# A two-layer block with product-key experts: gathered groups of rows shared out anew over the steps of the expert stage

## The chip, the cores and the metric

One core of a Trainium2 chip. Times are device microseconds of one execution. Where a profiled execution is used, its span (first to last instruction) and its own time are given. The engines are TensorE (PE in the profile, its weight loads PEld), VectorE (DVE), ScalarE (ACT), GpSimd (POOL) and SyncE (SP), each with its own instruction stream, run in order; they meet at semaphores.

## The reference

Two blocks follow each other on x [512 tokens, 1024]. Each has a mixer (gated linear attention in the first; retention and stick-breaking attention in the second) and then an expert layer (PEER). The change touches only how the expert layers are ordered in time:

```
q      = (h @ w_q)  per head and half                 # 8 heads, 2 halves of 128
top 16 of each half's scores against 128 sub-keys     # -> 256 candidates, best 16
expert = first_key * 128 + second_key                 # 16384 experts, 128 choices a token
act    = gelu(x . u[expert]) * softmax(best)
y      = sum over the 128 choices of act * v[expert]
```

u and v are float32 tables of 16384 x 1024 (64 MB each), one pair a layer.

## The kernel before

The four tiles of 128 tokens are treated in two ways. **Dense tiles** (2 and 3, 256 tokens): all of u and v is streamed once, as 128 blocks e of 128 experts (512 KB of u and 512 KB of v each, by SP). `first_product` (L747, matmuls at L753) multiplies block e of u with the tokens into one of two PSUM banks; ScalarE's `block_gelu` (L1206, L1211) takes it out; VectorE's `weigh_pair` (L1796, L1804) multiplies it with the tokens' gates for these experts, two blocks at a time; `second_product` (L757, L763) adds it to y in PSUM. The gates come from matmuls over one-hot rows: `gates_of_batch` (L773, L789) makes those of four tokens for a quarter of the blocks (64 batches a quarter). For each batch ScalarE's `hit_batch` (L1213, L1221 and L1224) spreads the second key, in quarter 0 every other batch is spread by VectorE's `second_keys` (L1786, L1792); for each four batches VectorE's `first_keys` (L1772, L1780 and L1782) spreads the first key, and ScalarE's `copy_gates` (L1226, L1231) copies four batches' result to SBUF.

**Gathered tiles** (0 and 1): each of a token's 128 choices is fetched by an indirect DMA from GpSimd (L2046, 128 rows of 4 KB), four choices a group. A u group (`score_rows`, L1851) takes four dot products on VectorE; `group_gelu` on ScalarE (L1234, L1237) follows; a v group (`add_rows`, L1862 and L1871) adds four weighted rows. There are 64 of each, 128 units in all a layer, u and v in turn; each kind has a ring of 6 rows, a slot of which is fetched again once VectorE has read it.

**The order** is written out by step tables. Before step 0 quarter 0's 64 batches run, with 24 first products (`EARLY`) and the first `FIRST_UNITS` units (one behind every fifth batch, `first_units`). Then 128 steps: at step e TensorE does first product e + 16 (`AHEAD`; from e = 8 until e = 111), second product e, and the batches up to `batches_due(e)` (192 are left). VectorE at step e does `weigh_pair(e + 4)` on even e, the first keys up to `spreads_due(e)`, one piece of the choice of tile 1's experts (steps 8 to 48), and the units up to `units_due(e)`. ScalarE at step e does the group gelus of VectorE's step e - 1, block gelu e + 15, the hits up to `batches_due(e + 1)` and the copies up to `copies_due(e)`. Hits have a ring of 4, the first keys' spreads a ring of 2, both freed by TensorE's batches. `first_product(e)` waits for block gelu e - 2.

`unit_table` (L135) gives `units_due`: from step 8 on, units in proportion to a share of TensorE's time in the step less VectorE's other work in it.

Of the kernel before, what the change touches and what calls it, by code (L numbers as in the profile page):

```python
# [23 lines left out]
NH, TOPK, NKEY = 8, 16, 128  # L24
# [8 lines left out]
BATCHES = ND // BATCH  # L33
WIDE = 16
WIDES = ND // WIDE
AHEAD = 16
EARLY = 24
# [6 lines left out]
GROUPS = SLOTS // RING  # L44
# [36 lines left out]
def by_scalar(q, n):  # L81

    return q > 0 or n % 2 == 0
# [13 lines left out]
PAIR_PIECES = 8  # L97
PIECES = 5 * PAIR_PIECES + 1
EXP_PIECE = PIECES - 5
FIRST_UNITS = 11  # L100
SHORT_UNITS = 5
LATER = (QUARTERS - 1) * BATCHES


def batches_due(e):

    return 0 if e < 0 else min(LATER, 2 * e + 4 + min(8, e // 2))


def spreads_due(e):  # L110

    return 0 if e < 0 else -(-batches_due(e + 1) // 4)


def copies_due(e):

    return 0 if e < 0 else min(LATER // 4, e // 2 + 3, batches_due(e + 1) // 4)
# [7 lines left out]
def pieces_due(e):  # L125

    return max(0, min(PIECES, e + 1 - (EARLY - AHEAD)))


def first_units(n):  # L130

    return max(0, min(FIRST_UNITS, n // 5))


def unit_table():  # L135

    room = []
    for e in range(NKEY - 2):
        pe = 3.45 * (1 + (EARLY <= e + AHEAD < NKEY)) + 0.37 * (batches_due(e) - batches_due(e - 1))
        other = 0.45 + 1.69 * (spreads_due(e) - spreads_due(e - 1)) + 1.25 * (pieces_due(e) - pieces_due(e - 1))  # L140
        room.append((pe, other))
    share = ((4 * GROUPS - FIRST_UNITS) * 5.15 + sum(v[1] for v in room)) / sum(v[0] for v in room)
    done, table = 0.0, []
    for pe, other in room[EARLY - AHEAD:]:
        done += max(0.0, share * pe - other)
        table.append(done)
    short = [FIRST_UNITS + (e + 1) * SHORT_UNITS // (EARLY - AHEAD) for e in range(EARLY - AHEAD)]
    return short + [short[-1] + round((4 * GROUPS - short[-1]) * v / done) for v in table]


UNITS = unit_table()


def units_due(e):

    return FIRST_UNITS if e < 0 else UNITS[min(e, len(UNITS) - 1)]


def unit(n):

    if n in (0, 4 * GROUPS - 1):
        return ("u", 0) if n == 0 else ("v", 2 * GROUPS - 1)
    return ("u", (n + 1) // 2) if n % 2 else ("v", n // 2 - 1)
# [49 lines left out]
def build(nc, a, out, mod_dram, x_dram, two_pi):  # L213
    with ExitStack() as ctx:
# [782 lines left out]
        def _(act):  # L997
# [208 lines left out]
            def block_gelu(layer, e):  # L1206
                at = layer * NKEY + e
                if e >= len(zg_first) + ZG:
                    act.wait_ge(blk_summed, at - ZG + 1)
                act.wait_ge(blk_done, at + 1)  # L1210
                nc.scalar.activation(zg(e), ps[4 + e % 2][:, 0:ND], ACT.Gelu).then_inc(blk_gelu, 1)  # L1211
# [41 lines left out]
            def unit_gelu(layer, u):  # L1253
                kind, g = unit(u)
                if kind == "u":
                    group_gelu(layer, g)

            def dense_acts(layer):
# [12 lines left out]
                for e in range(blocks_before(BATCHES - 5), EARLY):  # L1271
                    block_gelu(layer, e)
                for u in range(first_units(BATCHES - 6), FIRST_UNITS):
                    unit_gelu(layer, u)
# [92 lines left out]
        def _(dve):  # L1367
# [367 lines left out]
            def peer(layer):  # L1735
# [36 lines left out]
                def first_keys(q, m):  # L1772

                    at = (layer * QUARTERS + q) * WIDES + m
                    c = slice(m * WIDE, (m + 1) * WIDE)
                    if at >= 2:
                        dve.wait_ge(ga_used, 4 * (at - 1))
                    shape = [P, WIDE // BATCH, QA, BATCH]
                    of_keys = lambda v: v.rearrange("p (g t) -> p g t", t=BATCH).unsqueeze(2).to_broadcast(shape)
                    spreads(tt(hot_one, key_rows, of_keys(first_no[q][:, c]), ALU.is_equal))  # L1780
                    for r in range(3):
                        last = tt(hot[m % 2][:, r], hot_one, of_keys(g_part[:, r, c]), ALU.mult)  # L1782
                    last.then_inc(ga_ready, 1)
                    dve.wait_ge(ga_ready, at + 1)

                def second_keys(n):  # L1786

                    at = layer * QUARTERS * BATCHES + n
                    if at >= HITS:
                        dve.wait_ge(ga_used, at - HITS + 1)  # L1790
                    shape = [P, BATCH, P]
                    tt(hits[n % HITS].rearrange("p (j k) -> p j k", j=BATCH), keyno16.unsqueeze(1).to_broadcast(shape),  # L1792
                       second_no[:, n * BATCH:(n + 1) * BATCH].unsqueeze(2).to_broadcast(shape), ALU.is_equal)\
                        .then_inc(hit_by_vector, 1)

                def weigh_pair(e):  # L1796

                    at = layer * NKEY + e
                    q, j = divmod(e, QA)
                    if j == 0:  # L1800
                        dve.wait_ge(ga_copied, (layer * QUARTERS + q + 1) * WIDES)
                    dve.wait_ge(blk_gelu, at + 2)
                    z = zg_pair(e)
                    tt(z, z, gates[q % 2][:, j:j + 2, :, :], ALU.mult).then_inc(blk_ready, 2)  # L1804

                chooser = tile_experts(1)
                for n in range(BATCHES):
                    if n % 4 == 0:
                        first_keys(0, n // 4)
                    if not by_scalar(0, n):  # L1810
                        second_keys(n)
                    for u in range(first_units(n - 1), first_units(n)):
                        run_unit(layer, u)
                for e in range(0, WEIGHED, 2):
                    weigh_pair(e)
                for e in range(NKEY):
# [18 lines left out]
            def run_unit(layer, n):  # L1835
                kind, g = unit(n)
                if kind == "u":
                    score_rows(layer, g)
                else:
                    add_rows(layer, g)  # L1840
                    if g % GROUPS == GROUPS - 1:
                        finish_tile(layer, g // GROUPS, y)

            def score_rows(layer, g):

                at = layer * 2 * GROUPS + g
                for b in range(RING):
                    n = RING * at + b
                    row = ur[n % ROWS]
                    dve.wait_ge(u_in[n % ROWS], 16 * (n // ROWS + 1))  # L1850
                    nc.vector.tensor_tensor_reduce(out=row, in0=row, in1=hn[:, g // GROUPS, :], scale=1.0, scalar=0.0,  # L1851
                                                   op0=ALU.mult, op1=ALU.add, accum_out=a8[g % 2][:, b:b + 1])\
                        .then_inc(u_free, 1)

            def add_rows(layer, g):

                at = layer * 2 * GROUPS + g
                if layer == 0 and g == 0:
                    dve.wait_ge(ada_stored, 16 * 12)
                c = g // GROUPS * SLOTS + g % GROUPS * RING  # L1860
                dve.wait_ge(act_out, at + 1)
                tt(c8[g % 2], g8[g % 2], gate[:, c:c + RING], ALU.mult).then_inc(c8_ready, 1)  # L1862
                dve.wait_ge(c8_ready, at + 1)
                for b in range(RING):
                    n = RING * at + b
                    row = vr[n % ROWS]
                    dve.wait_ge(v_in[n % ROWS], 16 * (n // ROWS + 1))
                    if g % GROUPS == 0 and b == 0:
                        last = ts(y, row, c8[g % 2][:, b:b + 1], None, ALU.mult)
                    else:  # L1870
                        last = stt(y, row, c8[g % 2][:, b:b + 1], y, ALU.mult, ALU.add)  # L1871
                    last.then_inc(v_free, 1)
                    dve.wait_ge(v_free, n + 1)

            def finish_tile(layer, t, y):

                if t in GATHERED:
                    dve.wait_ge(gathered_x_back, 32 * (layer + 1))
                if layer == 0:
                    tt(x[:, t, :], x[:, t, :], y, ALU.add).then_inc(x_ready, 1)  # L1880
                    dve.wait_ge(x_ready, t + 1)
                else:
                    dve.wait_ge(gate_in, 16)
                    step(tt(ysum, y, rows[:, 2, :], ALU.mult))
                    tt(x[:, t, :], x[:, t, :], ysum, ALU.add).then_inc(out_ready, 1)
                    dve.wait_ge(out_ready, t + 1)

            peer(0)
            dve.sem_inc(dve_to_act, 1)

# [129 lines left out]
            for t in range(NT):  # L2020
# [7 lines left out]
                rstd(1, D, t)  # L2028
                normed_tile(t, rows[:, 1, :], mod[:, 3, :])
            peer(1)  # L2030


# [59 lines left out]
```

## Time and profile before

| | us |
|---|---|
| median of 3 runs | 3321.93 (3318.65 to 3331.39) |
| the profiled execution's own time | 3318.72 |
| its span | 3316.9 |
| busy: PE, DVE, ACT, POOL | 3078.7, 2420.3, 1340.9, 1326.1 |
| HBM read | 921.87 MB, 280 GB/s over the span |

The span has two expert stages: layer 0's steps from 691.4 to 1628.8 us and layer 1's from 2367.5 to 3306.3 us, each behind about 110 us in which quarter 0's gates are made. PE's busy time counts matmuls from start to end, and they overlap, so 100% is a queue without gaps and not the peak rate. PEclk is the granted clock as a share of full speed. A row such as `[1.07 <-ACT big L1211]` says that the engine sat idle for 1.07 us before and what ended it.

### The profile page before, as it was taken

What the parts mean: (1) busy time and instruction counts of PE and PEld (TensorE: products, weight loads), DVE (VectorE), ACT (ScalarE), POOL (GpSimd) and SP (SyncE); (2) the same over time, 40 slices, a digit from 0 to 9 for tenths busy, and PEclk for the clock granted to TensorE, in tenths of its full rate; (3) what the DMA queues carried; (4) which work ended last, traced back from release to release, by engine and by line L of the source; (5) the groups of instructions that cost most, each with busy time, mean ns of one, the idle gap of its engine ahead of it and who ended that gap; (6) DMA issues with size and microseconds to landing.
All of it is one profiled execution on the core that took longest, in us unless ns stands there. A gap on an engine that the chain in (4) does not pass through costs nothing. (4 is left out here: it accounts for less than half of the span.)

```text
span 3316.9 us, 45880 instructions
## 1 busy us (share of the span) xinstructions
PE 3078.7 (93%) x16440; PEld 2049.9 (62%) x16440; DVE 2420.3 (73%) x5311; ACT 1340.9 (40%) x3417; POOL 1326.1 (40%) x1040
## 2 busy tenths in 40 slices
PE   7999899889999999988699999998899999999887
PEld 2466488656666666655344565787666666666553
DVE  5874459988889878777721253499888888878777
ACT  3232122786555555400111153226866565555000
POOL 0000000655556767766300000005456656767664
PEclk9999999999999999999899989999999999999999
DMA  8510261989999999999812101518799999999998
GB/s 302 181 51 26 95 228 65 347 291 364 374 371 376 409 409 409 409 408 409 332 57 82 49 22 38 195 67 310 276 359 376 384 353 409 409 409 409 409 409 351
DMA packets 282682, 931.22 MB, mean 281 GB/s; under 512 B 31804, under 2 KB 32460, under 8 KB 281944
## 3 DMA queue, kind: packets, MB, share of 16 engines
q0 software_dynamic: 147840, 536.96, 41.6%
q1 hardware_dynamic: 134616, 391.34, 31.3%
q8 instruction: 131, 2.15, 0.3%
q14 instruction: 95, 0.78, 0.1%
HBM read 921.87 MB, written 6.32 MB: 280 GB/s over the span
## 5 line engine op out<-in xcount | busy, mean ns | idle before, releaser
L753 PE MATMUL psum<-hT,mod 128*128 128x256 f32 x4096 | 969.8, 392 | 64.0 <-ACT big L1211 38.6
L753 PEld LDWEIGHTS psum<-hT,mod 128*128 128x128 f32 x4096 | 782.2, 195 | 189.7 <-issue 86.7
L1221 ACT ACTIVATE levels<-key_numbers,hT 128x128 bf16<-128x128 f32 x1792 | 566.7, 389 | 138.0 <-PE psum L789 137.5
L1871 DVE SCALAR_TENSOR_TENSOR tmp<-w,small,tmp 128x1024 f32<-128x1024 f32 x339 | 435.7, 1285 | 82.3 <-DMA w<-in_peer_v,tmp 37.8
L2046 POOL DMA_INDIRECT w<-in_peer_u,tmp x172 | 236.4, 1374 | 584.2 <-DVEq L1702 447.3
L1851 DVE CUSTOM_DVE_ANT_0 w<-w,hn 128x1024 f32<-128x1024 f32 x342 | 408.7, 1224 | 73.5 <-DMA w<-in_peer_down,tmp 36.2
L2046 POOL DMA_INDIRECT big<-in_peer_down,tmp x86 | 117.5, 1366 | 720.0 <-DVEq L1702 633.7
L763 PE MATMUL psum<-rows,big 128*128 128x512 f32 x768 | 344.2, 592 | 3.3 <-DVE big L1804 3.3
L789 PEld LDWEIGHTS psum<-x,levels 128*128 128x128 bf16 x6144 | 225.7, 101 | 164.8 <-issue 100.9
L1224 ACT ACTIVATE levels<-levels 128x512 bf16<-128x512 bf16 x448 | 282.2, 630 | 14.2
L789 PE MATMUL psum<-x,levels 128*128 128x32 bf16 x6144 | 236.9, 196 | 50.5 <-DVE levels L1792 25.7
L1231 ACT ACTIVATE big<-psum 128x512 f32<-128x512 f32 x128 | 137.3, 1072 | 343.3 <-PE psum L789 323.1
L2046 POOL DMA_INDIRECT w<-in_peer_down,tmp x170 | 224.5, 1321 | 117.0 <-DVE small L1851 73.7
L2046 POOL DMA_INDIRECT w<-in_peer_v,tmp x172 | 215.5, 1253 | 130.0 <-DVE tmp L1871 88.0
L2046 POOL DMA_INDIRECT w<-in_peer_up,tmp x170 | 214.0, 1259 | 119.6 <-DVE tmp L1871 78.5
L1871 DVE SCALAR_TENSOR_TENSOR tmp<-big,small,tmp 128x1024 f32<-128x1024 f32 x169 | 217.1, 1285 | 40.4 <-DMA big<-in_peer_up,tmp 18.1
L1237 ACT ACTIVATE small<-small 128x4 f32<-128x4 f32 x128 | 26.0, 203 | 537.1 <-DVE small L1851 537.0
L763 PEld LDWEIGHTS psum<-rows,big 128*128 128x128 f32 x768 | 145.6, 190 | 154.1 <-issue 150.0
L1851 DVE CUSTOM_DVE_ANT_0 big<-big,hn 128x1024 f32<-128x1024 f32 x170 | 203.9, 1223 | 30.9 <-DMA big<-in_peer_u,tmp 15.3
L763 PE MATMUL psum<-srow,big 128*128 128x512 f32 x384 | 173.0, 593 | 2.3 <-DVE big L1804 2.3
L763 PE MATMUL psum<-tmp,big 128*128 128x512 f32 x384 | 172.6, 592 | 0.0
L740 PE MATMUL psum<-hT,w 128*128 128x256 f32 x640 | 144.8, 379 | 0.0
(328 smaller groups left out, 4179.7 us busy)
## 6 DMA issues: line engine op xcount, KB each, us to landing
mod<-in_uT SPq DMA_DIRECT2D x256, 512.0 KB, 6.8
rows<-in_peer_v SPq DMA_DIRECT2D x64, 512.0 KB, 6.8
rows<-in_peer_up SPq DMA_DIRECT2D x64, 512.0 KB, 6.8
w<-in_w_in SPq DMA_DIRECT2D x14, 2048.0 KB, 8.5
srow<-in_peer_v SPq DMA_DIRECT2D x32, 512.0 KB, 6.9
tmp<-in_peer_v SPq DMA_DIRECT2D x32, 512.0 KB, 6.8
srow<-in_peer_up SPq DMA_DIRECT2D x32, 512.0 KB, 6.8
tmp<-in_peer_up SPq DMA_DIRECT2D x32, 512.0 KB, 6.8
```

Of the source, the lines that this page charges most:

```text
L740: last = nc.tensor.matmul(bank[:, 0:2 * P], w[:, k, c * P:(c + 1) * P], hT[:, k, tokens], start=k == 0, stop=k == KC - 1)
L753: last = nc.tensor.matmul(ps[4 + e % 2][:, 0:ND], ub[e % UV][:, k, :], hT[:, k, ND:SEQ], start=k == 0, stop=k == KC - 1)
L763: last = nc.tensor.matmul(y_dense[n][:, c * 512:(c + 1) * 512], zg(e)[:, n * P:(n + 1) * P], vb[e % UV][:, c * 512:(c + 1) * 512], start=e ...
L789: last = nc.tensor.matmul(ps[6 + n // 4 % 2][:, t * QA:(t + 1) * QA], hits[n % HITS][:, j * P:(j + 1) * P], hot[n // 4 % 2][:, r, n % 4, : ...
L1221: last = nc.scalar.activation(hits[n % HITS][:, j * P:(j + 1) * P], keyno, ACT.Abs, bias=nibT[:, n * BATCH + j:n * BATCH + j + 1])
L1224: nc.scalar.activation(hits[n % HITS], hits[n % HITS], ACT.Relu, scale=-1.0, bias=1.0).then_inc(hit_ready, 1)
L1231: nc.scalar.activation(gates[q % 2][:, :, 2 * m:2 * m + 2, :], ps[6 + m % 2].rearrange("p (j i a) -> p a j i", a=QA, i=8), ACT.Copy).then_ ...
L1237: nc.scalar.activation(g8[g % 2], a8[g % 2], ACT.Gelu).then_inc(act_out, 1)
L1851: nc.vector.tensor_tensor_reduce(out=row, in0=row, in1=hn[:, g // GROUPS, :], scale=1.0, scalar=0.0, op0=ALU.mult, op1=ALU.add, accum_out= ...
L1871: last = stt(y, row, c8[g % 2][:, b:b + 1], y, ALU.mult, ALU.add)
L2046: nc.gpsimd.indirect_dma_start(ring[n % ROWS], None, table, bass.IndirectOffsetOnAxis(idx[:, c:c + 1], 0))\
```

## The change

Three edits. The lead of the batches over two a step grows by one each four steps and not each two, so it reaches 8 at step 32 and not 16. One more unit is placed ahead of step 0; a loop is added for those that the batches' loop leaves over. And the units from step 8 on are shared out by a new measure: the smaller of TensorE's time in the step less VectorE's other work (with 0.53 us for weighing, not 0.45), and TensorE's time less 1.28 us for each dense block that is transferred.

```diff
-FIRST_UNITS = 11
+FIRST_UNITS = 12
...
-    return 0 if e < 0 else min(LATER, 2 * e + 4 + min(8, e // 2))
+    return 0 if e < 0 else min(LATER, 2 * e + 4 + min(8, e // 4))
...
 def unit_table():
-    room = []
-    for e in range(NKEY - 2):
-        pe = 3.45 * (1 + (EARLY <= e + AHEAD < NKEY)) + 0.37 * (batches_due(e) - batches_due(e - 1))
-        other = 0.45 + 1.69 * (spreads_due(e) - spreads_due(e - 1)) + 1.25 * (pieces_due(e) - pieces_due(e - 1))
-        room.append((pe, other))
-    share = ((4 * GROUPS - FIRST_UNITS) * 5.15 + sum(v[1] for v in room)) / sum(v[0] for v in room)
+    short = [FIRST_UNITS + (e + 1) * SHORT_UNITS // (EARLY - AHEAD) for e in range(EARLY - AHEAD)]
     done, table = 0.0, []
-    for pe, other in room[EARLY - AHEAD:]:
-        done += max(0.0, share * pe - other)
+    for e in range(EARLY - AHEAD, NKEY - 2):
+        blocks = 1 + (e + AHEAD < NKEY)
+        pe = 3.45 * blocks + 0.37 * (batches_due(e) - batches_due(e - 1))
+        other = 0.53 + 1.69 * (spreads_due(e) - spreads_due(e - 1)) + 1.25 * (pieces_due(e) - pieces_due(e - 1))
+        done += max(0.0, min(pe - other, pe - 1.28 * blocks))
         table.append(done)
-    short = [FIRST_UNITS + (e + 1) * SHORT_UNITS // (EARLY - AHEAD) for e in range(EARLY - AHEAD)]
     return short + [short[-1] + round((4 * GROUPS - short[-1]) * v / done) for v in table]
...
                     for u in range(first_units(n - 1), first_units(n)):
                         run_unit(layer, u)
+                for u in range(first_units(BATCHES - 1), FIRST_UNITS):
+                    run_unit(layer, u)
                 for e in range(0, WEIGHED, 2):
                     weigh_pair(e)
```

What the tables give, worked out from the code:

| after step | units before | after | batches before | after |
|---|---|---|---|---|
| ahead of 0 | 11 | 12 | 0 | 0 |
| 8 | 17 | 18 | 24 | 22 |
| 16 | 24 | 26 | 44 | 40 |
| 24 | 30 | 34 | 60 | 58 |
| 32 | 37 | 42 | 76 | 76 |
| 48 | 51 | 57 | 108 | 108 |
| 90 | 97 | 102 | 192 | 192 |
| 111 | 121 | 122 | 192 | 192 |
| 125 | 128 | 128 | 192 | 192 |

## Rows read from the trace of the kernel before

**Rows 1.** The page's 40 slices of the span: GB/s moved in each.

```profile
GB/s 302 181 51 26 95 228 65 347 291 364 374 371 376 409 409 409 409 408 409 332 57 82 49 22 38 195 67 310 276 359 376 384 353 409 409 409 409 409 409 351
```

**Rows 2.** Stretches of layer 0's stage: busy us of engines, clock, DMA share, GB/s.

```profile
580.00:691.40 111.40, 92.21 (x1038) 80.02 (x1037) 104.50 (x191) 78.41 (x198) 68.96 (x54) 0.94 0.91 336
691.40:740.40 49.00, 42.73 (x334) 24.17 (x334) 40.38 (x71) 45.63 (x122) 26.27 (x19) 0.97 0.75 270
740.40:1056.60 316.20, 311.86 (x1982) 214.74 (x1981) 271.39 (x596) 195.20 (x519) 182.91 (x141) 1.00 0.97 370
...
808.70:871.00 62.30, 62.30 (x398) 42.93 (x397) 57.14 (x131) 41.33 (x112) 41.14 (x32) 1.00 1.00 391
...
1056.60:1391.40 334.80, 328.52 (x2018) 225.70 (x2017) 274.83 (x396) 185.05 (x498) 236.18 (x179) 0.99 1.03 408
1391.40:1565.70 174.30, 154.25 (x537) 100.84 (x536) 128.35 (x162) 9.39 (x34) 113.14 (x96) 0.94 1.03 409
```

**Rows 3.** Waits, total us, times, longest; first 1056.6 to 1391.4, then to 1628.8.

```profile
PE psum L753 <- ACT big L1211: 6.3, 2, 3.2
...
PE psum L753 <- ACT big L1211: 10.4, 2, 8.7
PE psum L753 <- ACT hT L1211: 9.7, 2, 8.7
PE psum L763 <- DVE big L1804: 3.3, 4, 2.0
...
ACT small L1237 <- DVE small L1851: 212.6, 16, 16.3
```

**Rows 4.** Waits of VectorE from 740.4 to 1056.6 us.

```profile
DVE x L1780 <- PE psum L789: 34.0, 12, 6.9
```

**Rows 5.** Timeline of TensorE: start, us, line, operation, count; regular steps and the last product.

```profile
921.57 3.70 PE L753 MATMUL psum<-hT,mod 128*128 128x256 f32 x16
925.10 3.60 PE L763 MATMUL psum<-tmp,hT 128*128 128x512 f32 x8
928.53 0.93 PE L789 MATMUL psum<-x,levels 128*128 128x32 bf16 x24
929.30 3.70 PE L753 MATMUL psum<-hT,mod 128*128 128x256 f32 x16
...
1405.95 3.60 PE L763 MATMUL psum<-rows,big 128*128 128x512 f32 x8
...
1412.84 3.60 PE L763 MATMUL psum<-rows,big 128*128 128x512 f32 x8
...
1621.59 3.60 PE L763 MATMUL psum<-tmp,big 128*128 128x512 f32 x8
```

**Rows 6.** Waits of TensorE, 740.4 to 1056.6, and timelines around one of them.

```profile
PE psum L753 <- ACT hT L1211: 2.6, 2, 1.5
PE psum L753 <- ACT big L1211: 1.8, 2, 1.1
...
762.01 3.69 PE L753 MATMUL psum<-hT,mod 128*128 128x256 f32 x16 [1.07 <-ACT big L1211]
...
760.60 1.06 ACT L1231 ACTIVATE big<-psum 128x512 f32<-128x512 f32 x1 [5.00 <-PE psum L789]
```

**Rows 7.** Timeline of TensorE: a late stall.

```profile
1303.70 5.38 PE L753 MATMUL psum<-hT,mod 128*128 128x256 f32 x16 [3.04 <-ACT big L1211]
```

**Rows 8.** Timeline of VectorE: start of a u group, end of the v group behind it.

```profile
788.65 1.20 DVE L1851 CUSTOM_DVE_ANT_0 w<-w,hn 128x1024 f32<-128x1024 f32 x1
...
796.51 2.60 DVE L1871 SCALAR_TENSOR_TENSOR tmp<-w,small,tmp 128x1024 f32<-128x1024 f32 x2
```

**Rows 9.** Timeline of TensorE in step 0: one of seven batches that wait.

```profile
699.40 0.55 PE L789 MATMUL psum<-x,levels 128*128 128x32 bf16 x12 [1.28 <-ACT levels L1224]
```

**Rows 10.** Timeline of VectorE: the last spreads of quarter 0 and the first weighing.

```profile
683.74 1.29 DVE L1792 TENSOR_TENSOR levels<-key_numbers,hT 128x512 bf16<-128x512 bf16 x2
689.26 3.00 DVE L1804 TENSOR_TENSOR x<-x,big 128x512 f32<-128x512 f32 x3 [4.22 <-issue]
```

## The prediction

> **What bounds the kernel now.** I read the slices first [rows 1]: from slice 8 and again from slice 29 GB/s climbs from about 350 to 409 and stays there. These are the two expert stages, one per layer, some 1,050 us each of the 3317. The table by stage [rows 2] splits layer 0's stage at its steps: start of step 0 (691.4), 8 (740.4), 48 (1056.6), just before step 91 (1391.4), step 112 (1565.7) and the end (1628.8). In steps 8 to 47 TensorE is busy throughout and DMA moves 370 GB/s; from step 48 on DMA moves 408 to 409, two thirds of a layer's stage, and TensorE falls to 154 of 174 us. So the first third is paced by TensorE with transfers to spare, and the rest by transfers. The waits say the same [rows 3]: after step 91 ScalarE waits 212.6 of 237 us for VectorE's last scored row (it runs the group's gelu in order, ahead of the block gelu that frees TensorE's bank), and TensorE then waits for ScalarE's block gelu. VectorE itself waits for rows to land. From step 8 to 47 there are no such waits; there VectorE waits 34.0 us for TensorE's gate batches [rows 4].
>
> **TensorE's chain, to price things.** A step with two products and two batches is 7.73 us (921.57 to 929.30), one without batches 6.89 (1405.95 to 1412.84), a second product alone 3.43 (925.10 to 928.53), a batch 0.385 (half of what stands between 928.53 and 929.30) [rows 5]. From step 8: 83 x 7.73 + 21 x 6.89 + 16 x 3.43 + 2 odd batches x 0.385 = 842 us, so it could end at 740.4 + 842 = 1582.4. Its last second product begins at 1621.59 [rows 5] and ends at 1625.1. Of the 42.7 us lost, 4.4 are four short stalls before step 17 (2.6 and 1.8 in all, the longest 1.5 [rows 6]); 38.3 come late: 29.7 us of waits [rows 3], the rest slow matmuls after them: 16 take 5.38 us after a wait of 3.04, against 3.69 after 1.07 [rows 6, 7].
>
> **The share of groups.** A group of four gathered rows is 4 x 128 x 4 KB = 2.097 MB, 5.13 us at 409 GB/s; a dense block is 0.524 MB. The code's tables give, after step 48, 77 groups before and 71 after the change. Needed at 409 GB/s, against TensorE's time:
> - steps 49 to 90: before 46 groups, 140.5 MB, 343.6 us against 324.7: 18.9 over; after 45: 13.8 over.
> - steps 91 to 111: before 24 groups, 72.4 MB, 176.9 against 144.7: 32.2 over; after 20: 11.7 over.
> - steps 112 on: before 7, 1.4 over; after 6, 3.7 under.
>
> Before 52.5 over, of which 38.3 were lost: 14.2 is swallowed by the lead that the engines have over each other. After 21.8 over; less 14.2 leaves 7.6. That is -30.7 us, six groups times 5.13. Bounds: nothing gained (if the six can't be moved earlier) and -38.3 (if no late stall is left).
>
> Can steps 8 to 47 take five groups more (34 become 39; the sixth runs before step 0)? DMA: 370 GB/s x 316.2 us is 117.0 MB, plus 10.5 is 127.5 MB in about 326 us (TensorE's longer chain, below): 391 GB/s, under the 408 to 409 that it holds for 509 us [rows 2]. VectorE: a pair of groups takes from 788.65 to 796.51 + 2.60, so 5.2 us each, a little of it other work between them [rows 8]; 271.4 busy us plus 5 x 5.2 are 297 of 326, and the extra comes out of the 34.0 us for which it waits for TensorE anyway [rows 4]. It fits, with 9% to spare, tightest around step 16 (57.1 of 62.3 us now in steps 16 to 23 [rows 2]; one to two groups more fill it).
>
> At this place the Trainium skill speaks against the change: DMA: Bandwidth & Descriptors, section "Where 436 GB/s comes from", says that for transfers between HBM and SBUF the memory side binds at about 358 GB/s per core. By that the middle (370) would be full already, and the groups moved would only move the queue. The trace disagrees with 409 held for 509 us [rows 2], so the sum doesn't use it; a softer ceiling of that kind is rival 3.
>
> **The gates' lead.** Half of the extra batches now comes later: two fewer up to step 7 (19, not 21) and at step 8 (22, not 24). Before step 8 TensorE's batches wait for ScalarE, which spreads one each 1.83 us (a batch of 0.55 behind a wait of 1.28) and is busy 45.6 of 49 us [rows 2, 9]. Two fewer: -3.7 us; between that and 0, if something else paces; I take -3.7.
> The price: a gate copy on ScalarE waits for the fourth batch of its set. Where that batch falls in TensorE's next step, the copy (1.06 us) and the gelu behind it end after TensorE wants the bank: at 760.60 the copy runs after 5.00 us of waiting, and TensorE's next product starts 1.07 us late [rows 6]. The code's tables give this for 4 copies from step 8 on before (the products that follow, in steps 11, 13, 14 and 16, are the four stalls of 4.4 us in all), and for 13 after, up to step 32. At 1.1 each: +9.9 us. Bounds: the least and the most of the four, 0.7 (1.8 less the 1.1 beside it) and 1.5 [rows 6], give +4.7 to +15.1. Batches only deferred cost nothing more: 0.385 us each wherever they stand. VectorE's spreads follow the batches and are as many.
>
> **The twelfth group.** It is a scored one (u), at batch 60; the added loop behind the batches is then empty, so it does nothing. Its four rows (4.6 us) stand ahead of VectorE's spreads for batches 61 and 63, which end at 685.0 now [rows 10], and TensorE wants them from 686.4. After: 61 at about 689.1, 63 at 689.7, the batches end 2.2 us later than now, and with them the copy and the first weighing (689.26), before which VectorE idles 4.22 us [rows 10]. +2.2 us; bounds 0 (cover of 4.22) and 4.6. Queued behind it: ScalarE's group gelu and the first hits. Its gather of 2.1 MB lies where DMA moves 336 GB/s [rows 2].
>
> **Sum.** Per layer -30.7 - 3.7 + 9.9 + 2.2 = -22.3 us. From the bytes: unused now 316.2 x (409 - 370)/409 = 30 us in steps 8 to 47, after 326 x (409 - 391)/409 = 14; that is -16, with -5.1 for the group ahead and -1.5 for step 8 coming earlier: -22.6. I take -20 (VectorE at 91% will not fit without friction). Layer 1's slices, from 29 on, are those of layer 0 [rows 1], so the same again: -40 us. The profiled execution took 3318.72 (span 3316.9, 1.8 around it): 3279; the median of the runs is 3.2 above it: 3282.
>
> **Rivals.**
> 1. No late stall is left: singles instead of the double-group steps (steps 77, 87, 94 and 102 take two; the long stalls come one to three steps later, as at 1303.70 before step 80 [rows 7]) end them altogether, and with them the slow matmuls. -38.3 + 8.4 = -30 a layer: 3262. For it: the new table has no double after step 79. Against: 21.8 us of transfers are still over.
> 2. VectorE becomes the bound in steps 8 to 47: its waits for TensorE [rows 4] are ordering and don't shrink. 297 + 37 = 334 against 326: 8 us a layer go, and 2 more for the late product: -10 a layer: 3302. For it: steps 16 to 23 at 92% [rows 2].
> 3. Transfers top out near what steps 8 to 47 show (370 to 391 GB/s [rows 2]) while TensorE is fed too; no byte moves early. Then 9.9 + 2.2 - 3.7 = +8 a layer: 3338. Against: 409 stands beside a TensorE busy 328 of 335 us.
> 4. The other side: the 13 copy stalls grow with VectorE's fuller queue. One mechanism: ScalarE's copy waits a step, VectorE's late group behind it makes the stall 3 us, and matmuls go slow as at 1303.70 [rows 7]: 3.04 + 1.69 = 4.7 each, 13 x 4.7 - 4.4 = +57, less 30.7 and 1.5: +25 a layer: 3372. It decides from 13 c - 4.4 = 32.2, that is c = 2.8 us a stall; the four seen are 0.7 to 1.5.
>
> **How the numbers follow.** Forecast 0.50, rival 1 0.17, rival 2 0.18, rival 3 0.05, rival 4 0.06, and 0.04 that all cancel near no change. Under 0.5% (16.6 us) from 3322 a measurement can't tell from no change: faster is below 3305, slower above 3339. Faster: forecast, rival 1, most of rival 2: 0.82. Same: 0.11. Slower: 0.07. The range takes rival 1 and rival 2 in: 3256 to 3308.
>
> **What would show it.** Right: GB/s about 390 in steps 8 to 47 and TensorE's late waits under 15 us a layer; step 8's second product within 3 us of 740.4; some 13 waits of TensorE for ScalarE of about 1.1 us up to step 32; ScalarE's 212.6 us wait for VectorE far smaller; first weighing 2 us later. Wrong: VectorE waiting for landings before step 48, 5.38 us products before step 32, or DMA under 380 in the middle with the late stalls unchanged.

## The result and the profile after

Median of five runs 3300.36 us (3296.57 to 3302.62) against 3321.93 before (3318.65 to 3331.39, five runs): ratio 0.9928, 95% interval 0.9915 to 0.9941. The forecast was 3282 us and a gain of 40 us. The gain is 21.6 us between the medians, and 24 us by the ratio: as forecast in direction and inside the range, but little more than half in size. The profiled executions have spans of 3300.2 and 3316.9 us (before).

First GB/s in the page's 40 slices after the change, to lay beside [rows 1]:

```profile
GB/s 293 193 42 36 96 209 79 339 291 395 379 380 395 403 409 409 409 409 409 314 56 83 36 35 39 179 77 296 283 391 375 370 398 400 409 408 409 409 409 336
```

Then layer 0's stage after, cut at the same steps as in [rows 2] (starts of step 0, 8, 48, just before 91, 112, and TensorE's end); the columns are busy us of the engines with counts, granted clock, DMA share, GB/s:

```profile
697.30:743.90 46.60, 41.59 (x309) 23.30 (x308) 36.93 (x57) 42.15 (x114) 23.60 (x19) 0.96 0.76 269
743.90:1074.00 330.10, 314.12 (x2006) 216.13 (x2006) 296.40 (x636) 197.84 (x530) 203.08 (x159) 1.00 1.00 387
1074.00:1407.20 333.20, 327.31 (x2018) 224.75 (x2017) 274.87 (x392) 184.31 (x498) 230.39 (x180) 0.99 1.02 408
1407.20:1566.40 159.20, 152.91 (x537) 100.08 (x536) 112.43 (x144) 9.25 (x32) 100.72 (x83) 0.98 1.03 409
1566.40:1621.50 55.10, 55.10 (x129) 24.13 (x127) 38.89 (x45) 2.04 (x6) 19.11 (x16) 1.00 0.82 324
```

Steps 8 to 47 now move 387 GB/s (370 before) and VectorE is busy 296.4 us in them (271.4): the five groups went in, at almost exactly the 127.5 MB and 297 us of the forecast (387 x 330.1 = 127.8 MB). But the stretch takes 330.1 us, not the 326 forecast and the 316.2 before. The last stretch, 55.1 us at 324 GB/s, is new too: TensorE doesn't wait there any more, and the transfers idle for (409 - 324)/409 x 55.1 = 11 us.

TensorE's waits after: first in 743.9 to 1074.0, then in 1074.0 to 1407.2, then from 1407.2 on, there with ScalarE's wait for VectorE (total us, times, longest). They answer to [rows 6] and [rows 3]:

```profile
PE psum L750 <- ACT big L1208: 12.3, 10, 1.5
PE psum L750 <- ACT hT L1208: 3.6, 3, 1.5
...
PE psum L750 <- ACT big L1208: 4.6, 1, 4.6
...
PE psum L750 <- ACT big L1208: 6.3, 3, 3.1
ACT small L1234 <- DVE small L1850: 166.4, 12, 18.1
```

There are 13 short waits, 15.9 us, where 4 took 4.4; each layer has them. The late waits fell from 29.7 us to 12.2 in layer 0 (4.6 and 6.3 as shown, and 1.3 once before batches at 1334, for which the profile names no releaser) and from 30.3 to 13.7 in layer 1, and ScalarE's wait for VectorE's last row from 212.6 to 166.4 us.

What each layer's stage took, stretch by stretch, read off the timelines of TensorE and VectorE (first row of u scored, starts of second products 0, 8, 48, 91 and 112, end of the last; last column: the last group's end against TensorE's):

| us | first u row to step 0 | steps 0-7 | 8-47 | 48-90 | 91-111 | 112-127 | last group |
|---|---|---|---|---|---|---|---|
| before, layer 0 | 100.7 | 48.9 | 316.2 | 342.5 | 166.7 | 59.4 | +3.6 |
| before, layer 1 | 100.7 | 48.9 | 317.9 | 340.2 | 169.3 | 58.3 | +4.1 |
| changed, layer 0 | 104.7 | 46.7 | 330.0 | 340.9 | 151.5 | 55.1 | -7.4 |
| changed, layer 1 | 104.7 | 46.7 | 331.7 | 339.7 | 152.9 | 55.1 | -7.1 |

Before, the last group ended a stage, now TensorE does, so a layer's stage is 9 us shorter, not 5: to TensorE's end 1034.4 became 1028.9 us and 1035.3 became 1030.7, and 3.6 to 4.1 us of a group behind it are gone. Both stages together give 17.7 us, and the end of layer 1 another 2.5 (tile 1 is finished ahead, not behind). Of that 3.5 us are lost again in work that the change does not touch, 1.7 ahead of layer 0's first u row and 1.8 between the stages; so the two spans differ by 16.7.

### The profile page after: what moved, and what is told of

Read it like the earlier page. It is cut to its first block and busy times, and to the rows that moved or that the text cites. A ratio compares the mean times of both kernels' runs of the same rounds, so it can differ in the third digit from the quotient of the medians.

```text
span 3300.2 us, 45872 instructions
## 1 busy us (share of the span) xinstructions
PE 3081.3 (93%) x16440; PEld 2052.6 (62%) x16440; DVE 2418.4 (73%) x5311; ACT 1338.2 (41%) x3417; POOL 1304.0 (40%) x1040
## 3 DMA queue, kind: packets, MB, share of 16 engines
q8 instruction: 131, 2.15, 0.3%
## 5 line engine op out<-in xcount | busy, mean ns | idle before, releaser
L1221 ACT ACTIVATE levels<-levels 128x512 bf16<-128x512 bf16 x448 | 282.2, 630 | 14.2
L1870 DVE SCALAR_TENSOR_TENSOR tmp<-big,small,tmp 128x1024 f32<-128x1024 f32 x169 | 217.2, 1285 | 43.8 <-DMA big<-in_peer_up,tmp 22.3
L2045 POOL DMA_INDIRECT w<-in_peer_up,tmp x170 | 203.1, 1195 | 115.0 <-DVE tmp L1870 76.0
```

What stands on the lines that cost most here:

```text
L1221: nc.scalar.activation(hits[n % HITS], hits[n % HITS], ACT.Relu, scale=-1.0, bias=1.0).then_inc(hit_ready, 1)
L2045: nc.gpsimd.indirect_dma_start(ring[n % ROWS], None, table, bass.IndirectOffsetOnAxis(idx[:, c:c + 1], 0))\
```

## The experiments

All ratios are to the kernel before, timed in the same round on the same chip. The changed kernel was timed in the first round only, with the kernel before at 3321.93 us; in the later rounds that kernel took 3322.83 to 3325.34. Differences to the changed kernel, and between rounds, are therefore good to a few us. Two theories share most runs: A, each edit is a term of its own on TensorE's chain, and the lead's short waits cost what they take; B, transfers pace the stage, so what TensorE waits early is free; further ones (C to F) are named where they come up.

### One part at a time

The twelfth unit alone:

```diff
-FIRST_UNITS = 11
+FIRST_UNITS = 12
```

> The kernel before with the twelfth unit alone. Theory A (each edit is a term of TensorE's chain): step 0 starts about 4 us later a layer, as in the changed kernel (2.2 of waiting batches and 1.6 to 1.7 of slow matmuls behind them), and one group less (5.1 us of transfers) is late after step 48: 3320, 0 to -4 us against before. Rival B (the stage is bound by its transfers, what TensorE waits early is free): only the moved transfer counts, -5 us a layer, 3312.

Measured: 3323.16 against 3325.20 us, ratio 0.9992 (0.9983 to 1.0001): nothing that can be told from no change. In the stretches both halves of the term are there: 104.7 us to step 0 and not 100.7 (both layers), and 563.8 us from step 48 to TensorE's end where 568.5 were, one group's 5 us. This is theory A.

The gates' lead alone:

```diff
-    return 0 if e < 0 else min(LATER, 2 * e + 4 + min(8, e // 2))
+    return 0 if e < 0 else min(LATER, 2 * e + 4 + min(8, e // 4))
```

> The kernel before with the slower lead of the gates alone. Theory A: about 2 us a layer won up to step 8, 13 short waits of 1.2 us instead of 4 and two deferred batches (+12) up to step 32, late waits lowered by a few us at most: +8 us a layer, 3338. Rival B: the transfers catch up during the short waits and the late waits shrink by as much: no change, 3322.

Measured: 3348.80 us, ratio 1.0071 (1.0058 to 1.0085), 23.6 us slower. Steps 0 to 7 take 46.6 us (-2.3), steps 8 to 47 333.4 in both layers (+17.2 and +15.5), and from step 48 to TensorE's end 568.7 us against 568.5 in layer 0: nothing of the early loss comes back late. That is against B, and worse than A expected, which put +12 us on steps 8 to 47: two products a layer, in steps 17 and 28, are slow behind their wait here (5.38 us and not 3.69), which is 3.4 us. TensorE's waits in steps 8 to 47 are those of the changed kernel to a tenth, 12.3 us in 10 and 3.6 us in 3. The stretch as a window:

```profile
739.30:1072.70 333.40, 317.43 (x2005) 218.40 (x2005) 273.66 (x605) 197.55 (x528) 180.35 (x143) 0.99 0.93 353
```

DMA moves 353 GB/s beside these waits, less than the 370 of before: the stretch got longer and the groups' table gave it no more groups to fetch.

The new share alone, with eleven units ahead of step 0 and the old lead (so its table is worked out with the old batches):

```diff
-        done += max(0.0, share * pe - other)
...
+        other = 0.53 + 1.69 * (spreads_due(e) - spreads_due(e - 1)) + 1.25 * (pieces_due(e) - pieces_due(e - 1))
+        done += max(0.0, min(pe - other, pe - 1.28 * blocks))
```

> The kernel before with the new share alone (eleven units ahead of step 0, the old lead). Theory A: the gain of the late steps (-17 to -20 us a layer, one group less moved than in the changed kernel) without the waits of lead and unit (about 14 us a layer together): 3286, below the changed kernel's 3300. Rival B: the transfers bound it as in the changed kernel, and one group more is late: 3300 to 3310.

Measured: 3280.44 us, ratio 0.9869 (0.9854 to 0.9884): 44.8 us faster, twice the whole change. Steps 8 to 47 take 316.2 and 317.9 us, to the tenth what they took before, although by the tables six groups more are in them (40, not 34; the changed kernel has 39, its sixth group standing ahead of step 0). VectorE's waits there, and the stretch:

```profile
DVE x L1777 <- PE psum L786: 6.9, 3, 3.6
DVE w L1850 <- DMA w<-in_peer_u,tmp: 6.2, 8, 1.3
...
740.60:1056.80 316.20, 311.86 (x1982) 214.76 (x1981) 293.33 (x620) 193.39 (x516) 208.94 (x160) 1.00 1.01 401
```

The 34.0 us that VectorE waited for TensorE [rows 4] have shrunk to 6.9: they were slack, not ordering, which is against rival 2 of the forecast. VectorE now waits for landings before step 48, 8.6 us in all (6.2 of them in the row above). And 401 GB/s are moved beside a TensorE that loses no more than before, which is against rival 3.

The changed kernel with the old lead:

```diff
-    return 0 if e < 0 else min(LATER, 2 * e + 4 + min(8, e // 4))
+    return 0 if e < 0 else min(LATER, 2 * e + 4 + min(8, e // 2))
```

> The changed kernel with the old lead. Theory A: four short waits instead of 13 in steps 8 to 32, 9 to 11 us a layer less: 3280. Rival B: VectorE and the transfers have less time before step 48 (the same groups in 316 and not 330 us), so the late waits grow by what the early ones lose: 3300.

Measured: 3282.71 us, ratio 0.9872 (0.9857 to 0.9887), 17.6 us under the changed kernel's median. Steps 8 to 47: 317.9 in both layers. The late stretches give back part: from step 48 on layer 0 takes 550.6 us against 547.5. This is A, with a few us a layer of B in it.

### The short waits, cured

Each copy of gates is put off by a step on ScalarE if its fourth batch is only made in TensorE's next step:

```diff
-    return 0 if e < 0 else min(LATER // 4, e // 2 + 3, batches_due(e + 1) // 4)
+    return 0 if e < 0 else min(LATER // 4, e // 2 + 3, batches_due(e) // 4)
```

> The changed kernel, with each gate copy put off by a step where its fourth batch is only made in TensorE's next step. Theory A (the 13 short waits are ScalarE's in-order copy): TensorE has no wait of 1.0 to 1.5 us in steps 8 to 32, steps 8 to 47 take 315 us and not 330, and a third or so of that comes back as late waits, since the transfers have less time: -9 to -11 us a layer, 3280. Rival B (transfers pace the stage, the short waits are free): steps 8 to 47 shorten, the late waits grow by the same 15 us, 3300.

Measured: 3268.25 us, ratio 0.9826 (0.9811 to 0.9841): 32 us under the changed kernel, more than A expected. TensorE has no wait at all in steps 8 to 47 of layer 0, which take 312.0 us; the stretch:

```profile
743.60:1055.70 312.10, 312.10 (x2006) 215.58 (x2005) 290.07 (x622) 195.74 (x515) 205.55 (x158) 1.00 1.02 404
```

Steps 0 to 7 fell too, to 44.0 us from 46.7 (the same pattern stands there four times, ahead of batches instead of products). From step 48 on layer 0 takes 551.5 us against 547.5: 4 of 21 us came back. So the mechanism is shown: ScalarE reaches a copy whose batch isn't made yet, and the gelu behind it frees TensorE's bank too late.

### The twelfth unit, moved

In the change the unit stands at batch 60, ahead of VectorE's spreads for batches 61 and 63. TensorE and VectorE of the changed kernel around it, answering to [rows 10]:

```profile
690.97 1.31 PE L786 MATMUL psum<-x,levels 128*128 128x32 bf16 x36 [2.15 <-DVE levels L1789]
692.12 5.31 PE L750 MATMUL psum<-hT,mod 128*128 128x256 f32 x16
697.27 3.60 PE L760 MATMUL psum<-rows,x 128*128 128x512 f32 x8
...
690.23 1.29 DVE L1789 TENSOR_TENSOR levels<-key_numbers,hT 128x512 bf16<-128x512 bf16 x2
693.46 2.96 DVE L1801 TENSOR_TENSOR x<-x,big 128x512 f32<-128x512 f32 x3 [1.94 <-issue]
```

Three batches wait 2.15 us, as forecast; but the product behind them takes 5.31 us and not 3.7 (687.91, 3.70 us, in the kernel before), and step 0 comes behind it. The unit moved behind the spreads, into the added loop:

```diff
-    return max(0, min(FIRST_UNITS, n // 5))
+    return max(0, min(FIRST_UNITS - 1, n // 5))
```

> The changed kernel with the twelfth unit behind the last spreads of quarter 0 instead of ahead of them. Theory A (the unit ahead of the spreads holds four batches, the first weighing and, by a slow first product, step 0: 4.0 us a layer): from the first unit to step 0 100.7 us and not 104.7, -8 us in all, 3292. Rival F (the 4 us are covered later, since ScalarE paces steps 0 to 7): step 8 stands where it stood, 3300.

Measured: 3299.05 us, ratio 0.9919 (0.9904 to 0.9934): 1.3 under the changed kernel, where I had expected 8. The way to step 0 is 100.7 and 100.9 us, as A has it, and steps 0 to 7 keep their 46.7. In the profiled execution, too, the span is only 0.8 us shorter. Two things take the gain back there. Steps 8 to 47 take 333.4 us in both layers and not 330.0 and 331.7: after the same wait the same product is slow in one execution and not in the other. And 4.4 us more stand outside the stages, ahead of layer 0's first u row and between the stages, where the two kernels are the same. The slow product, first in the changed kernel, then in this one, in step 17:

```profile
818.54 3.69 PE L750 MATMUL psum<-hT,mod 128*128 128x256 f32 x16 [1.46 <-ACT hT L1208]
```

```profile
816.80 5.38 PE L750 MATMUL psum<-hT,mod 128*128 128x256 f32 x16 [1.45 <-ACT hT L1208]
```

The granted clock is 1.00 in the first (818.50 to 822.20) and 0.67 on average over the second (816.80 to 822.00), so part of it ran at the lower of the two levels, half the speed. So a short wait costs 1.45 us, or 3.1; the order of the kernel alone does not say which. The loss of the unit's place is shown by the stretch; that the total shows nothing of it stays partly open.

### Both cures

```diff
-    return 0 if e < 0 else min(LATER // 4, e // 2 + 3, batches_due(e + 1) // 4)
+    return 0 if e < 0 else min(LATER // 4, e // 2 + 3, batches_due(e) // 4)
...
-    return max(0, min(FIRST_UNITS, n // 5))
+    return max(0, min(FIRST_UNITS - 1, n // 5))
```

> The changed kernel with both cures, unit behind the spreads and copies put off. Theory A (terms add): c_copies less 4.0 us a layer, 3260; steps 0 to 7 take 44 us, 8 to 47 312 us. Rival F: 3268.

Measured: 3263.12 us, ratio 0.9813 (0.9798 to 0.9828), 5 under the copies' cure alone, with 100.7 to 100.9, 44.0 and 312.0 us in the first three stretches. The kernel before was 2.5 us faster in this round than in that of the copies' cure, and the two intervals overlap, so the total alone does not show what the unit's place is worth. The stages do: to TensorE's end they take 1007.0 and 1009.3 us, and 1012.3 and 1013.3 with the copies' cure alone.

The same two with the old lead of the gates:

```diff
-    return 0 if e < 0 else min(LATER, 2 * e + 4 + min(8, e // 4))
+    return 0 if e < 0 else min(LATER, 2 * e + 4 + min(8, e // 2))
```

> The new share and twelve units ahead of step 0 with the old lead; the twelfth behind the last spread (where VectorE idles 4 us before the first weighing) and not ahead of it; copies put off as in the first run. Theory A: step 0 starts at 692 us instead of 694.5 to 697, no short waits (-4.4 us a layer), one group less late than with the share alone: 3270. Rival B: 3280, the late waits taking back what the early steps gain.

Measured: 3261.85 us, ratio 0.9810 (0.9796 to 0.9823). Steps 0 to 7 take 46.5 us, 8 to 47 311.3. A expected 3270; it came out 8 lower. Once copies wait for nothing, the lead is worth little either way: 44.0 + 312.0 against 46.5 + 311.3 us a layer, and no difference in the total.

### What the late waits are

Half of each v block is not transferred from block 52 on, in the kernel with the new share alone:

```diff
-                sp.dma_start(vb[e % UV], layer_v[layer][e * P:(e + 1) * P, :]).then_inc(vb_in[e % UV], 16)
+                n = D if e < 52 else D // 2
+                sp.dma_start(vb[e % UV][:, 0:n], layer_v[layer][e * P:(e + 1) * P, 0:n]).then_inc(vb_in[e % UV], 16)
```

> The new share alone, with only half of each v block transferred from block 52 on (the second half is what lies there, so the output is not the reference's): 0.26 MB a step less in the late steps, 49 us of transfers a layer. Theory A (late waits are bytes): VectorE stops waiting for landings, TensorE's late waits fall from about 21 us a layer (with the slow matmuls behind them) to under 3, steps 48 to the end take 532 to 535 us instead of 553. Rival C (late waits are order: two groups in one step hold ScalarE's gelu queue): the waits after the double steps 60, 72 and 84 stay, 4 to 9 us each.

Measured, in a single execution: 3236.26 us. Steps 48 to 90 take 332.5 us in both layers, 91 to 111 141.2, 112 to the end 55.1, which is TensorE's own time to the tenth (528.8; 553.2 with all the bytes), and the trace has no wait of TensorE in them. The windows:

```profile
1061.70:1394.30 332.60, 332.60 (x2066) 228.58 (x2066) 289.79 (x416) 187.87 (x506) 238.85 (x189) 1.00 1.02 402
1394.30:1535.40 141.10, 141.10 (x489) 92.69 (x488) 115.31 (x149) 9.23 (x31) 104.89 (x81) 1.00 1.03 404
```

The steps with two groups (60, 72 and 84) are still there and cost nothing, which is against rival C as a cause by itself. The late waits come from bytes, and not from the number of packets: both pages count 282682 packets, with 891.38 MB here and 931.22 MB in the share alone. Two things stay open. One part of A did not come: VectorE still waits for landings, 24.1 us in steps 91 to 111 against 42.4, so such waits alone do not say that TensorE loses anything. And with all the bytes a long wait can stand behind a double step (6.2 and 6.7 us in step 75 of the share alone, behind step 72); no run spreads these steps out at equal bytes. The run also corrects my chain: its minimum from step 48 is 528.8 us and not 532, because the last of its first products stands in step 111, and step 112 begins with a second product.

### Where the missing part went: the tail

The new share alone, with more room for groups from step 112 on (119 done after step 111, not 122):

```diff
-        done += max(0.0, min(pe - other, pe - 1.28 * blocks))
+        done += max(0.0, min(pe - other, pe - (1.28 * blocks if blocks == 2 else 0.45)))
```

> The new share alone, with room for 3.0 us and not 2.17 us of groups in each step from 112 on: 119 groups are done after step 111, not 122. Theory D (what the forecast missed is the tail: the groups end 5 to 9 us ahead of TensorE and the transfers idle there): the last group ends beside TensorE's end, the waits of 7 us around step 107 shrink, -4 to -8 us a layer against the share alone, 3268. Rival E (the tail idles because the last groups are bound by VectorE's order, not by their number): no change, 3280, or a later end.

Measured: 3279.37 us, ratio 0.9862 (0.9847 to 0.9877), 1 under the share alone. The expectation of 3268 did not come; the total is that of E. TensorE ends 7 us (layer 0) and 9 (layer 1) sooner, counted from the first u row: 1011.9 and 1011.1 us against 1019.0 and 1019.9. But the last group now ends 3.6 and 4.5 us behind TensorE, not 5.4 and 3.3 ahead of it, and tile 1 is finished behind that. The tail's transfers, first with 122 groups done (the share alone), then with 119:

```profile
1554.90:1610.00 55.10, 55.08 (x129) 24.11 (x127) 38.96 (x45) 2.04 (x6) 20.25 (x17) 1.00 0.83 325
```

```profile
1550.60:1607.70 57.10, 55.36 (x129) 24.08 (x127) 43.49 (x54) 0.82 (x4) 30.82 (x26) 1.00 0.98 387
```

So D is right that the tail has room for transfers, and wrong about the rest. The waits of steps 91 to 111 did not shrink (9.6 and 8.7 us in the share alone, 8.8 and 9.4 here); those of steps 48 to 90 did (7.5 and 8.2 to 1.0 and 1.4), for the new table has two groups fewer done by step 90 as well (100, not 102). And with three groups moved, the last group and the end of tile 1 behind it take back what TensorE won. With both cures (and the change's lead) and one group moved, 121 done after step 111:

```diff
-        done += max(0.0, min(pe - other, pe - 1.28 * blocks))
+        done += max(0.0, min(pe - other, pe - (1.28 * blocks if blocks == 2 else 0.95)))
```

> As the run before, with one group moved from before step 112 into the tail (121 done after step 111, not 122). Theory D (with 122 the last group ends 5 to 7 us ahead of TensorE, with 119 4 us behind it, and either costs): 121 ends nearer to TensorE's end and the wait before step 109 shrinks, -1 to -3 us a layer, 3256. Rival E: no change.

Measured: 3253.68 us, ratio 0.9786 (0.9769 to 0.9803), the fastest of all, 69 us under the kernel before, 47 under the changed one, and 9.4 under both cures alone in the same round, more than D expected. The stages take 1001.6 and 1005.0 us to TensorE's end, 5.3 and 4.3 less than with both cures alone, where one group's transfer is 5.1; the last group ends 2.1 and 0.3 behind it. The gain stands in steps 48 to 90 (344.9 in both layers before, 338.3 and 341.4 now) and not at the wait before step 109. The new table also puts its double steps elsewhere, and how much of the gain is due to that stays open. Layer 0:

```profile
738.70:1050.70 312.00, 312.00 (x2005) 215.28 (x2004) 293.61 (x630) 198.26 (x525) 208.87 (x159) 1.00 1.02 407
1050.70:1389.10 338.40, 334.44 (x2066) 229.78 (x2066) 277.54 (x397) 186.88 (x499) 228.40 (x179) 0.99 1.03 408
...
1540.40:1595.50 55.10, 55.10 (x129) 24.13 (x127) 42.54 (x52) 0.61 (x3) 27.48 (x23) 1.00 0.95 374
```

## Why the prediction came out at half its gain

Point by point, per layer, the forecast's terms and what the two profiles of the changed kernel give:

| term | forecast | layer 0, layer 1 |
|---|---|---|
| late waits, step 48 to TensorE's end | -30.7 | -21.1, -20.1 |
| copy waits, steps 8 to 47 | +9.9 | +13.8, +13.8 |
| two batches fewer, steps 0 to 7 | -3.7 | -2.2, -2.2 |
| twelfth unit, to step 0 | +2.2 | +4.0, +4.0 |
| the last group behind TensorE's end | not priced | -3.6, -4.1 |
| sum | -22.3 | -9.1, -8.6 |

**Bound and mechanism: right.** Transfers bound the steps from 48 on (the half blocks show it), five groups fit ahead of them, and VectorE's waits for TensorE gave the room. Rivals 2 and 3 fall with the share alone; rival 4 too, though it was nearer than I put it: it asked for 2.8 us a short wait and they cost 1.2, or 3.1 where the clock falls behind one. Rival 1 (no late wait left) did not come. Of the signs named ahead, the 387 GB/s, the late waits under 15 us and the 13 short waits came. Step 8 started 3.5 us after 740.4 and not within 3, and ScalarE's wait for VectorE fell only to 166.4 us. One product of 5.38 us before step 32, a sign of being wrong, stands in layer 1 (step 17); but before the change one stood there too (step 14), so this sign could not tell the two apart.

**The late term was priced at the wrong end.** I counted 52.5 us of transfers over before, 21.8 after, and let the same 14.2 be swallowed both times: -30.7 us, six groups' transfer. Up to the end of the *last group* that is what came. From the start of step 48 it took 572.2 and 571.9 us before and 540.1 and 540.6 after, 32.1 and 31.3 less; with half of each v block left out, 498.0 against 547.8 in layer 0, 49.8 less where 49 us of transfers were taken away. In all of these the core moves 400 to 406 GB/s from step 48 to the last group. But after the change TensorE ends the stage and not the last group, and TensorE's way to its end fell by 21.1 and 20.1 us only: 7.6 us over its own chain were to be left, and 18.7 are (547.5 against 528.8). 3.7 of the 30.7 us were room in the tail, after step 111, which nothing can use that is due before. The other part is that the 14.2 us are not swallowed in full a second time. The last group ends 7.4 us ahead of TensorE instead of 3.6 behind, 11 us in which the transfers idle although TensorE had waited for them in steps 82, 98 and 109. Moving three groups back into the tail returned 7 to 9 us to TensorE, but none to the total; moving one, with the cures, went the right way in the total too.

**The copy waits: right in place and number** (13, of 0.69 to 1.49 us), 15.9 us in all against 14.3 forecast, so 11.6 us more than before and not 9.9. Of the 13.8 us by which the stretch grew, the two deferred batches are another 0.8, which I called free though they had stood in ScalarE's time before step 8, not in TensorE's. The remaining 1.4 is, by my estimate, the overlap that a wait ends: a product starts 0.16 us before the modelled end of the batches ahead of it when it doesn't wait (928.53 + 0.93 against 929.30 [rows 5]), and there are nine waits more. The same sum gives the stretch without any wait: 316.2 - 4.4 - 4 x 0.16 + 0.8 = 312.0, as measured. Slow products have no part in it, with none in layer 0 before and after and one in layer 1 both times. The lead is the edit that eats the gain: alone it costs 23.6 us, and without it the changed kernel is 17.6 faster.

**Steps 0 to 7: 2.2 and not 3.7.** The copies ahead of their batch stand in these steps as well; with the copies cured they take 44.0 us, 4.9 under the 48.9 of before.

**The twelfth unit: the wait was right, 2.15 us.** The first product behind it, at the lower clock, was missing: 1.6 us. As one group less is late for it (5 us), the edit by itself is worth nothing either way.

**The ceiling.** The Trainium skill's figure (DMA: Bandwidth & Descriptors, section "Where 436 GB/s comes from"), about 358 GB/s where memory binds, is not what bounds this core: 407 and 408 GB/s stand from step 8 to step 90 of the best kernel.

## What to carry to other kernels

When one stretch of a stage waits for transfers and another has them idle, moving bytes is worth their transfer time, up to the point where the last consumer runs dry: look at the end of the stage too, say which of the two chains ends it, and balance them. An edit that spaces small work differently has to be checked against every in-order queue that touches it: here copies issued one step before their data was ready cost about half of what the moved groups had won. And where a change has three parts, run each alone; this one's best part was worth 45 us and was sold with one that cost 24.

## What the runs showed of the hardware

- After waits of the same length (1.45 and 1.46 us), behind the same products and batches, a product of 16 matmuls took 3.69 us in one execution and 5.38 in another; the granted clock was 1.00 in the one and 0.67 on average over the other. Behind 2.15 us it took 5.31, with a granted clock of 0.50 in its first 1.9 us. The length of the wait alone does not decide it. In the profiles of all these kernels 300 first products have a wait right before them: none of 154 was slow after less than 1.4 us, 17 of 50 after 1.44 to 1.49, 2 of 27 after 1.5 to 2 (nearly all of them in steps from 92 on), 11 of 20 after 2 to 3.23, and all 49 after 3.25 or more.
- TensorE without a gap (312.1 of 312.1 us), VectorE busy 93% and 404 GB/s of transfers, most of them gathered rows, went side by side in steps 8 to 47 of the kernel with the copies cured, and TensorE lost nothing by it.
